# Layer kernel on one core: x in eight portions, the first half tile of weights in two pieces

## The reference

```
proj = h @ w_in                      # q, k, v of 16 heads, latents, gates
y_a  = dilated_window_attention(q, k, v) @ a_w_out
y_b  = mla_attention(rms_norm(latents) @ (w_uq, w_ukv)) @ mla_w_out
h    = layer_norm(ALPHA * h + (g_a * y_a + g_b * y_b) @ w_out)
s1, s2 = (h @ w_query) against two tables of 128 keys, top 16 of each, top 16 of the sums
y    = sum over chosen experts of gate * gelu(h . expert_down[e]) * expert_up[e]
out  = layer_norm(ALPHA * h + y)
```

## Time and profile before

| | us |
|---|---|
| median of 3 runs | 2451.62 |
| lowest and highest | 2450.49 and 2454.09 |
| profiled execution | 2450.02 |
| its span, first to last instruction | 2448.3 |

### The profile page before, as it was taken

One profiled execution on the slowest core, in us unless ns is written; L12 is line 12 of the kernel. 1 busy time (PEld: TensorE's weight loads), 2 busy tenths in 40 slices (PEclk: granted clock), 3 DMA queues, 4 the chain that ended last, 5 costly groups with the idle time before them and its releaser, 6 DMA issues.

```text
span 2448.3 us, 49689 instructions
## 1 busy us (share of the span) xinstructions
PE 2421.9 (99%) x17932; PEld 2289.1 (93%) x17932; DVE 1487.1 (61%) x2443; ACT 1166.1 (48%) x1660; POOL 556.4 (23%) x379
## 2 busy tenths in 40 slices
PE   8999999999999999999999999999999999999997
PEld 8999999999999999999999999999888888888886
DVE  5555554646666667788888644444555555555556
ACT  5444444554444444655555544444444444444444
POOL 0000000000000000468888888800000000000000
PEclk9999999999999999999999999999999999999999
DMA  7666775554445655578888888876767777677764
GB/s 268 225 217 228 222 222 198 189 182 160 142 159 167 197 195 180 182 215 215 208 225 219 215 215 220 217 251 220 240 229 241 243 241 240 230 240 241 243 229 145
DMA packets 179848, 521.17 MB, mean 213 GB/s; under 512 B 52769, under 2 KB 52769, under 8 KB 179537
## 3 DMA queue, kind: packets, MB, share of 16 engines
q1 hardware_dynamic: 124128, 449.89, 56.3%
q0 software_dynamic: 51056, 53.83, 10.1%
q10 hardware_dynamic: 4608, 16.78, 1.7%
HBM read 484.64 MB, written 35.78 MB: 213 GB/s over the span
## 4 chain that ended last, share of the span: by engine, by line
PE 97%; DVE 2%; issue 1%; ACT 0%; DMA 0%; DVEq 0%; ACTq 0%
PE ps L1126 65%; PE ps L1330 28%; PE ps L1165 1%; PE ps L1180 1%; PE ps L1173 0%; PE ps L1167 0%; PE ps L1300 0%; PE ps L1181 0%; PE ps L1160 0%; DVE w_second L678 0%; DVE u_s L1079 0%; DVE u_s L1089 0%; DVE y_s L1066 0%; DMA res<-x_t 0%; DVE w_first L678 0%
## 5 line engine op out<-in xcount | busy, mean ns | idle before, releaser
L678 DVE TENSOR_TENSOR w_first<-raw,w_first 128x1024 fp32r<-128x1024 f32 x425 | 520.5, 1225 | 557.3 <-ACT w_first L388 540.4
L1126 PE MATMUL ps<-a_hi,w_first 128*128 128x256 f32 x3728 | 683.1, 279 | 11.0 <-DVE w_first L678 11.0
L1126 PE MATMUL ps<-a_hi,w_second 128*128 128x256 f32 x3728 | 672.5, 276 | 0.0
L1126 PEld LDWEIGHTS ps<-a_hi,w_first 128*128 128x128 f32 x3728 | 580.5, 188 | 11.9 <-issue 9.0
L1126 PEld LDWEIGHTS ps<-a_hi,w_second 128*128 128x128 f32 x3728 | 578.5, 188 | 0.1
L1126 PE MATMUL ps<-a_lo,w_first 128*128 128x256 f32 x1864 | 515.8, 277 | 0.0
L1126 PE MATMUL ps<-a_lo,w_second 128*128 128x256 f32 x1864 | 514.6, 276 | 0.0
L359 POOL DMA_INDIRECT g_dram<-gate_v,where x256 | 459.9, 1796 | 108.5 <-issue 78.5
L388 ACT ACTIVATE w_first<-raw 128x1024 fp32r<-128x1024 f32 x425 | 447.6, 1053 | 28.0 <-ACT act L606 17.7
L678 DVE TENSOR_TENSOR w_second<-raw,w_second 128x1024 fp32r<-128x1024 f32 x299 | 365.3, 1222 | 4.3 <-ACT w_second L388 4.2
L1126 PEld LDWEIGHTS ps<-a_lo,w_first 128*128 128x128 f32 x1864 | 351.1, 188 | 0.5
(11 more groups left out here) (210 smaller groups left out, 2880.3 us busy)
## 6 DMA issues: line engine op xcount, KB each, us to landing
raw<-stream SPq DMA_DIRECT2D x850, 512.0 KB
g_dram<-blank POOLq DMA_DIRECT2D x32, 512.0 KB, 6.2
a_dram<-act ACTq DMA_DIRECT2D x32, 512.0 KB
a_in<-a_dram POOLq DMA_DIRECT2D x32, 512.0 KB, 5.2
g_in<-g_dram POOLq DMA_DIRECT2D x32, 512.0 KB, 6.5
g_dram<-gate_v,where POOLq DMA_INDIRECT x256
res<-x_t SPq DMA_DIRECT2D x4, 512.0 KB, 6.8
ln_s<-ln POOLq DMA_DIRECT2D x1, 2048.0 KB, 7.7
```

The costliest lines, as they stand in the source:

```text
L678: dve.tensor_tensor(low, raw[:, s, :], high.bitcast(F32), ALU.subtract).then_inc(lo_ready, 1)
L1126: ins = pe.matmul(out, w, a, start=first and q == 0, stop=last and q == 2)
```

## The change

The transfer of x is cut from four quarters of 4 blocks to eight portions of 2 blocks (256 KB). The first half of tile 0 is cut in two pieces of 512 columns (256 KB), the first with a semaphore `piece_in` of its own. ACT rounds and DVE subtracts in the same portions, with new semaphores `piece_hi` and `piece_lo` for the first piece; `hi_ready` and `lo_ready` rise once, after the second piece. PE waits for `x_lo` ahead of every second block of tile 0, for `piece_lo` ahead of block 0 and for the whole half (`lo_ready`) ahead of block 4. The second half of tile 0 is issued behind portions 0 to 3 (blocks 0 to 7), where it was issued behind blocks 0 to 11. POOL waits for the last portion. Loops, tile order and everything behind the first tile are as they were.

```
-        for s in range(2):
-            x_part(2 * s)
-            sp.dma_start(raw[:, s, :], stream[s]).then_inc(raw_in[s], 16)
-            x_part(2 * s + 1)
+        x_part(0)
+        sp.dma_start(raw[:, 0, 0:PIECE], stream[0][:, 0:PIECE]).then_inc(piece_in, 16)
+        x_part(1)
+        sp.dma_start(raw[:, 0, PIECE:HALF], stream[0][:, PIECE:HALF]).then_inc(raw_in[0], 16)
+        x_part(2)
+        x_part(3)
+        sp.dma_start(raw[:, 1, :], stream[1]).then_inc(raw_in[1], 16)
+        for q in range(4, X_PARTS):
+            x_part(q)
...
-        for q in range(4):
+        for q in range(X_PARTS):
+            o = slice(X_BLOCKS * q, X_BLOCKS * q + X_BLOCKS)
             act.wait_ge(x_in[q], 16)
-            act.activation(a_hi[:, 4 * q:4 * q + 4, :], res[:, 4 * q:4 * q + 4, :], ACT.Copy).then_inc(x_hi, 1)
-            if q in (0, 2):
-                hi(Tile(0), (q // 2,))
+            act.activation(a_hi[:, o, :], res[:, o, :], ACT.Copy).then_inc(x_hi, 1)
+            if q == 0:
+                act.wait_ge(piece_in, 16)
+                act.activation(w_hi[0][:, 0:PIECE], raw[:, 0, 0:PIECE], ACT.Copy).then_inc(piece_hi, 1)
+            if q == 1:
+                act.wait_ge(raw_in[0], 16)
+                act.activation(w_hi[0][:, PIECE:HALF], raw[:, 0, PIECE:HALF], ACT.Copy).then_inc(hi_ready, 1)
+            if q == 3:
+                hi(Tile(0), (1,))
...
-                half_ready(t, hf)
+                if before is first_blocks and hf == 0:
+                    pe.wait_ge(piece_lo, 1)
+                else:
+                    half_ready(t, hf)
...
+        def x_block(kk):
+            pe.wait_ge(x_lo, kk // X_BLOCKS + 1)
+            if kk == PIECE // P:
+                half_ready(Tile(0), 0)
```

More of the change, by code:

```diff
@@ L65 @@
 HALF = 1024
+PIECE = HALF // 2
+X_PARTS = 8
+X_BLOCKS = KD // X_PARTS
 WIDE = 384
@@ L229, in build @@
     acc_free = [sem("acc_free0"), sem("acc_free1")]
-    x_in, par_in, keys_in, ln2_in = [sem(f"x_in{q}") for q in range(4)], sem("par_in"), sem("keys_in"), sem("ln2_in")
+    x_in, par_in, keys_in, ln2_in = [sem(f"x_in{q}") for q in range(X_PARTS)], sem("par_in"), sem("keys_in"), sem("ln2_in")
     par_in2 = sem("par_in2")
+    piece_in, piece_hi, piece_lo = sem("piece_in"), sem("piece_hi"), sem("piece_lo")
     x_hi, x_lo, vt_ready, vt_mm, v_ready = sem("x_hi"), sem("x_lo"), sem("vt_ready"), sem("vt_mm"), sem("v_ready")
@@ L296, in x_part @@
         def x_part(q):
-            sp.dma_start(res[:, 4 * q:4 * q + 4, :], x_t[:, 4 * q:4 * q + 4, :]).then_inc(x_in[q], 16)
-        for s in range(2):
-            x_part(2 * s)
-            sp.dma_start(raw[:, s, :], stream[s]).then_inc(raw_in[s], 16)
-            x_part(2 * s + 1)
+            o = slice(X_BLOCKS * q, X_BLOCKS * q + X_BLOCKS)
+            sp.dma_start(res[:, o, :], x_t[:, o, :]).then_inc(x_in[q], 16)
+        x_part(0)
[7 more added lines that the diff above has]
+            x_part(q)
         for s in range(2, 4):
@@ L324, in _ @@
     def _(pool):
-        pool.wait_ge(x_in[3], 16)
+        pool.wait_ge(x_in[X_PARTS - 1], 16)
         pool.dma_start(small[:], small_in).then_inc(par_in, 16)
@@ L711, in _ @@
         dve.memset(stat[:, 14:15], LN_EPS).then_inc(eps_ok, 1)
-        for q in range(4):
+        for q in range(X_PARTS):
+            o = slice(X_BLOCKS * q, X_BLOCKS * q + X_BLOCKS)
             dve.wait_ge(x_hi, q + 1)
[L715 to L718, removed]
+            dve.tensor_tensor(a_lo[:, o, :], res[:, o, :], a_hi[:, o, :].bitcast(F32), ALU.subtract).then_inc(x_lo, 1)
+            if q == 0:
+                dve.wait_ge(piece_hi, 1)
+                dve.tensor_tensor(w_lo[0][:, 0:PIECE], raw[:, 0, 0:PIECE], w_hi[0][:, 0:PIECE].bitcast(F32), ALU.subtract).then_inc(piece_lo, 1)
+            if q == 1:
+                dve.wait_ge(hi_ready, 1)
+                dve.tensor_tensor(w_lo[0][:, PIECE:HALF], raw[:, 0, PIECE:HALF], w_hi[0][:, PIECE:HALF].bitcast(F32),
+                                  ALU.subtract).then_inc(lo_ready, 1)
+            if q == 3:
+                lo(Tile(0), (1,))
         def head_a(h, first):
@@ L1181, in pv @@
             pe.matmul(ps_o[:, P:T], v_s[:, 1, :], p_t[:, T:384], start=False, stop=True, skip_group_check=True).then_inc(o_ready, 1)
-        def quarters(sem):
-            return {4 * q: lambda q=q: pe.wait_ge(sem, q + 1) for q in range(4)}
+        def x_block(kk):
+            pe.wait_ge(x_lo, kk // X_BLOCKS + 1)
+            if kk == PIECE // P:
+                half_ready(Tile(0), 0)
+        first_blocks = {kk: lambda kk=kk: x_block(kk) for kk in range(0, KD, X_BLOCKS)}
         def head_a(h, first):
             t = Tile(T_QKVG, h, 4) if not first else Tile(0)
-            full(t, a_hi, a_lo, quarters(x_lo) if first else None)
+            full(t, a_hi, a_lo, first_blocks if first else None)
             if not first:
```

## The result

The change costs time: 2455.98 us median (2455.15 to 2457.30) against 2451.55 (2449.77 to 2454.09), twenty runs each, a ratio of 1.0019 with the interval 1.0013 to 1.0026. The forecast was 2451.7 and its range ended at 2454.0, so the time lies outside it, on the slow side.

The account below looks back on a forecast made before the run. The prediction took matmuls to bound the kernel (97% of 2448.3 us) and transferred bytes its start. The early start would shrink to +0.08 us at tile 1: 2451.62 + 0.08 = 2451.7 us, range 2449.0 to 2454.0.

Parts of the forecast that it names:

- Part 1: Kernel start: with smaller first transfers PE's first matmul comes at 6.80 us, 2.2 us before 9.03.
- it does not do what it says: Rival at the start: weight piece 0 lands late, PE starts at up to 8 us, total still 2451.7; chance 0.10.
- Part 2: Rest of tile 0: PE pauses from 11.0 to 12.8, block 15 ends near 15.5 instead of 16.20; 0.7 us left.
- PE stays slow over the pause: Rival in tile 0: matmuls stay slow behind the pause, tile 1 starts 0.8 later than before, total 2452.4; chance 0.14.
- Part 3: Tile 1's start: same bytes ahead, 2 KB lines add +0.3; PE at 16.28, +0.08 us, between 15.94 and 16.51.
- The sum: Whole kernel: profiled 2450.02 plus 0.08 is 2450.1; carrying the median's 1.60 over gives 2451.7 us.
- Everything behind the start shifts as one block: After the start: PE is fed ahead of need, so all later work moves by the same amount as the start.
- each transfer pays for itself: Rival at the start: five more transfers each cost fixed time, at most 3.2 us, 16 in all, 2468; chance 0.02.
- The range: Whole kernel's median: mechanisms span 2449.4 to 2452.4; with the spread of runs on top, 2449.0 to 2454.0 us.

Follow-up runs that it names:

- tile_one: `x_blocks` with tile 1's first half rounded and subtracted in two pieces and ACT's long loop 128 instructions behind its old place; 2451.35 us against 2451.01, ratio 1.0000.
- after_far: Changed kernel with 124 empty semaphore increments on ACT, so 128 instructions are added ahead of its long loop; 2453.33 us against 2451.12 before, ratio 1.0009.
- the four pairs: Pairs of kernels differing only in DRAM layout: portions of x, in some also weight pieces, contiguous instead of strided; differences 2.45, 2.2, 2.3 and 1.7 us.
- x_blocks: Changed kernel with only the eight portions of x contiguous in DRAM, weight pieces left as they were; 2453.53 us against 2451.12 before, ratio 1.0009.
- act_four: Kernel before with four semaphore increments that nobody waits for added on ACT in the latents stage; 2453.57 us against 2451.26, ratio 1.0011.

## Why the prediction was wrong, point by point

**Part 1, the first matmul.** Forecast 6.80, found 5.89. The mechanism held, and the sum was too long in one term: the landing. I let weight piece 0 land at 5.39; ACT took it at 4.44, right behind x portion 0 at 3.82. Before, ACT took the quarter of twice the size at 5.39. The prices of the pieces held: 0.63 on ACT (taken 0.60), 0.69 on DVE (taken 0.69). The rival *it does not do what it says* fell with it.

**Part 2, the rest of tile 0.** The pause was forecast as one of 1.8 us before block 8, with block 15 ending near 15.5. The pauses came as 2.42 us before block 4 (at 11.21) and 0.63 before block 8 (at 14.77), and tile 0 ended near 17.8. Two terms failed: the landings interpolated at 413 GB/s, where 244 were reached, and the 3.07 us of slow stretch, which is not a constant. The rival *PE stays slow over the pause* described what `tile_one` and `after_far` did; it was priced at +0.8 and cost `after_far` 1.5 us between its tile 1 and that of the changed kernel.

**Part 3, tile 1.** This is the step that failed at the start. I priced the 2 KB lines from the stores of the output, the only 2 KB lines in the trace, at 0 to +0.59 us. They measured +2.11 on the landing (15.66 against 13.55) and up to +1.93 on PE, and by the medians of the four pairs the layout costs 1.7 to 2.45 us of the whole. Those stores and these loads share the length of a line in a partition but not the layout in DRAM, and `x_blocks` shows that the layout carries it: with it mended, tile 1 starts at 15.87, near the other end that Part 3 gave (15.94).

**The sum.** "Everything behind the start shifts as one block" was the second step that failed, twice over. PE's wait of 1.15 us at 1059 us went away, and at 1212 us the wait grew from 0.8 to 3.8 us; neither has to do with the start. The sum had no term for instructions added to ACT's program. Four of them measured +2.3 us (`act_four`), more than anything that the prediction weighed except the rival *each transfer pays for itself*. That one fell: `x_blocks` has the thirteen transfers and lands tile 1's half at 13.40, as early as the kernels with eight (13.36 to 13.74). The fixed time that the rival takes from the Trainium skill is from a section on transfers issued by GpSimd; these are issued by SP.

**The range.** Its top, 2454.0, was the top of the runs of before. With a start worth up to +2 and an unseen term it should have reached 2456. By 0.2% the most likely outcome, no change, came true only barely: the ratio is 1.0019 and its interval reaches 1.0026. That is luck rather than insight, since neither loss was in the forecast.

## What to carry to other kernels

Cutting the transfers cost nothing by their count here, but it did by where their bytes lie: lay the source out anew in blocks of the new size, or price the cut from a load with the same lines and the same distance between them. A change that adds or removes even a few instructions ahead of a long loop can shift the time by 0.1% either way, so put the same number of empty ones into the old kernel before believing a difference of that size, and look at the count of instruction packets on the page. The start of one profile can be off by more than the change is worth (1.4 us here), so read it beside other kernels that have the same start. A start that comes sooner is worth only as much as the next piece of work that is bound by bytes can move.

## What the runs showed of the hardware

- With x in 2 KB lines out of every 16 KB the DMA engines were busy (share 0.94) at 244 GB/s from 4.0 to 8.5 us; with the same bytes in unbroken blocks of 256 KB they moved 336, and with 4 KB lines out of every 16 KB 373.
- ACT stood 4.3 to 5.2 us at the turn of its loop with 4 or 32 instructions more ahead of it, against 1.0 to 1.05 with 0, 64, 96 or 128 more. The issue of one store in the same loop took 2.3 to 3.5 us with 0 or 128 more, and 0.40 with 4 to 96.
- TensorE ran its first matmuls 0.213 us apart for 3.1 to 5.9 us where no pause cut them, and for 3.4 to 13.2 us where pauses did, while the granted clock read 1.00. Behind a pause of 3.8 us at 1212 us the granted clock did fall, to 0.57 over 4 us, at a cost of 1.4 us.
